# Seven half-size products per pair of gate tiles, in a transformer trunk on one Trainium2 core

## The reference, cut to what matters

```
for l in range(DEPTH):
    h = rmsnorm(x, norm_mix[l])
    z = h @ w_in[l]                       # 1024 -> 3608 columns
    q, kc, vc, ks, vs, kw, vw, nsa_g, u, g_a, g_s = jnp.split(z, split_at, axis=-1)
    o_a = nsa_mixer(q, ...)               # three attention branches: compressed, selected, window
    o_b = s5_mixer(u, ...)                # diagonal state space, then a GLU
    merged = jax.nn.sigmoid(g_a) * (o_a @ proj_nsa[l]) + jax.nn.sigmoid(g_s) * (o_b @ proj_s5[l])
    x = x + merged @ w_out[l]
    x = x + hier_moe(rmsnorm(x, norm_ffn[l]), ...)   # 32 experts, 96 matrices of 2 MB in each layer
```

## Time and profile before

| What | Value |
|---|---|
| Time, median of 3 runs (lowest, highest) | 1862.13 us (1861.97, 1865.38) |
| Span of the profiled execution | 1861.1 us, 21432 instructions |
| TensorE busy | 1689.1 us, 91% |
| VectorE busy | 553.4 us, 30% |
| ScalarE busy | 391.6 us, 21% |

### The profile page before, as it was taken

The page is one execution under the profiler, slowest core; times in us unless marked ns, Lnnn a source line. Parts: engine busy times, 40 slices in busy tenths (PEclk is TensorE's granted clock), DMA queues, the critical chain, the costliest instruction groups (busy, mean ns, idle before and its releaser), DMA issues. The chain is left out here.

```text
span 1861.1 us, 21432 instructions
## 1 busy us (share of the span) xinstructions
PE 1689.1 (91%) x7466; PEld 817.6 (44%) x7466; DVE 553.4 (30%) x1678; ACT 391.6 (21%) x967; POOL 81.9 (4%) x157
## 2 busy tenths in 40 slices
PE   8999999999998778788999999999999987778788
PEld 6664444445443323233477644444544432333233
DVE  4872345435000000000378713463340000000003
ACT  3323344111111111111132234440111111110111
POOL 1000000000010000000000000000001100000000
PEclk9999999999999999998999999999999998999999
DMA  5641110463999999999938211004659999999997
GB/s 168 157 132 46 33 36 23 181 249 127 398 427 426 428 426 427 426 427 427 389 104 223 66 46 46 24 23 181 249 197 412 427 426 427 425 427 428 425 427 332
DMA packets 121903, 496.39 MB, mean 267 GB/s; under 512 B 42036, under 2 KB 78900, under 8 KB 94160
## 3 DMA queue, kind: packets, MB, share of 16 engines
q1 hardware_dynamic: 109584, 472.75, 64.0%
q0 software_dynamic: 8928, 16.52, 2.4%
q10 hardware_dynamic: 3296, 5.84, 0.8%
HBM read 489.25 MB, written 30.47 MB: 279 GB/s over the span
## 5 line engine op out<-in xcount | busy, mean ns | idle before, releaser
L1104 PE MATMUL bank<-arena 128*64 128x512 f32 x2176 | 692.5, 622 | 93.4 <-DMA arena<-in_expert_up 31.7
L1104 PEld LDWEIGHTS bank<-arena 128*64 128x64 f32 x2176 | 229.6, 143 | 358.8 <-issue 358.6
L2034 DVE SCALAR_TENSOR_TENSOR arena<-bank,halves,arena 128x512 f32<-128x512 f32 x32 | 24.0, 751 | 814.6 <-PE bank L1104 814.6
L779 PE MATMUL bank<-hT,arena 128*128 128x512 f32 x512 | 262.0, 611 | 4.1 <-ACT arena L1344 3.5
L1104 PE MATMUL bank<-h,arena 128*64 128x512 f32 x320 | 140.0, 614 | 24.2 <-DMA arena<-in_expert_gate 9.7
L1104 PE MATMUL bank<-spare_slot,arena 128*64 128x512 f32 x320 | 134.7, 618 | 28.9 <-DMA arena<-in_expert_gate 9.0
L754 PE MATMUL bank<-arena,hT 128*128 128x256 f32 (+1 forms) x512 | 118.0, 387 | 3.1 <-DMA arena<-in_w_in 2.3
L1104 PE MATMUL bank<-hT,arena 128*64 128x512 f32 x256 | 120.7, 627 | 0.0
L997 PE MATMUL bank<-arena,hT 128*128 128x512 f32 x256 | 115.0, 597 | 0.0
L779 PEld LDWEIGHTS bank<-hT,arena 128*128 128x128 f32 x512 | 83.4, 192 | 52.2 <-issue 44.3
L754 PEld LDWEIGHTS bank<-arena,hT 128*128 128x128 f32 x512 | 95.6, 190 | 19.4 <-DVE hT L1570 2.7
(11 more groups left out here) (366 smaller groups left out, 1638.8 us busy)
## 6 DMA issues: line engine op xcount, KB each, us to landing
arena<-in_expert_up SPq DMA_DIRECT2D x48, 2048.0 KB, 34.1
arena<-in_expert_gate SPq DMA_DIRECT2D x44, 2048.0 KB, 36.1
arena<-in_expert_down SPq DMA_DIRECT2D x44, 2048.0 KB, 40.4
arena<-in_w_in SPq DMA_DIRECT2D x26, 1024.0 KB, 7.1
spare_slot<-in_expert_gate SPq DMA_DIRECT2D x8, 2048.0 KB, 30.0
h<-in_expert_gate SPq DMA_DIRECT2D x8, 2048.0 KB, 31.6
hT<-in_expert_up SPq DMA_DIRECT2D x8, 2048.0 KB
spare_slot<-in_expert_down SPq DMA_DIRECT2D x8, 2048.0 KB, 37.9
```

The source lines that it names most:

```text
L779: r = pe.matmul(bank[:, FB, :], lhs, rhs, start=(k == 0), stop=last)
L1104: r = pe.matmul(dst[CAP * e:CAP * e + CAP, :], moving[:, k, CAP * e:CAP * e + CAP], w, start=(k == 0), stop=(k == n - 1))
L2034: STT(hid, bank[:, 3, :], slot_root, hid, ALU.mult, ALU.mult).then_inc(act_ready, 1)
```

## The change

Four of the sixteen gate tiles (`PLAIN = 2` pairs) stay as they are. The other twelve are taken as six pairs (`FAST = 6`). For a pair the weights are a 2x2 block matrix (low and high half of the 1024 rows by first and second tile), the tokens a 2x2 block matrix (low and high rows by early and late 256 tokens), and the product is made by Strassen's scheme in Winograd's form: seven products, each of four matmuls of 128x128 against 256 tokens, in place of sixteen matmuls against 512.

- Sums of tokens (`token_sums`, four, 128x1024 each) are made once per layer by VectorE, three into the dead query part of `h`, one in place in `hT`.
- Sums of weights (`weight_sum`, four per pair, 128x512 each) are made by VectorE ahead of the pair.
- The products run in four stages, (1, 6), (2, 7), (4, 5), (3), each one filler group in the bank. After stage 0 ScalarE copies the bank into `fast_p` (in `spare_slot`) and VectorE adds one half into the other; after the others VectorE adds the bank to what is there (`half_sums`: 512 columns after stage 1, 512 and 256 after stage 2, 256 after stages 0 and 3), and right behind it makes the next pair's weight sum s + 1.
- The tanh of a fast pair is taken later, by ScalarE from SBUF (`tanh_fast`), and the merge waits for it (`gate_ready`).
- `fill` counts in units of a 256-column product; 100 are done ahead of the loop (nine groups), 48 + 98 in it, 2 behind it. The 24 entries of `FILL_AT` are chosen so that every group in the loop but the last ends in the call in front of `scores(n + 1)`.
- The fast pairs' chunks alternate between ring slots 0 and 2; slots 1 and 3 hold the sums of weights. `load(0)` and `load(1)` of the experts wait for all half sums as well.

```
-FILL = [("gate", i) for i in GATES[:8]] + [("z", m) for m in range(4)] + [("gate", i) for i in GATES[8:]]
-FILL_AHEAD = 52
-FILL_AT = [5, 4, 3, 2]
+STAGES = ((1, 6), (2, 7), (4, 5), (3,))
+FILL = [("gate", i) for i in GATES[:2 * PLAIN]]
+FAST_STAGES = [("fast", j, s) for j in range(FAST) for s in range(4)]
+FILL += FAST_STAGES[:18] + [("z", 0)] + FAST_STAGES[18:20] + [("z", m) for m in range(1, 4)] + FAST_STAGES[20:]
+RING_AT = [0, 1, 2] + [3, 3] + [3, 2] + [0, 2] * (FAST // 2) + [1, 0, 2]
+FILL_AT = [8, 6, 2, 6, 6, 6,
...
+            def filled_before(i):
+                g = FILL[i - 1]
+                if i and g in BY_ACT:
+                    pe.wait_ge(fill_evac, BY_ACT[g])
+                elif i:
+                    pe.wait_ge(half_sum, BY_DVE[g])
...
                 for n in range(len(UNITS)):
-                    rest = fill(FILL_AT[UNITS[n][0]] - 1, one_group=True)
+                    fill(FILL_AT[n])
                     if n + 1 < len(UNITS):
                         scores(n + 1)
-                    fill(rest)
                     values(n)
...
+                def half_sums(j, s):
+                    m = fast_gates(j)
+                    both = bank[:, FB, :]
+                    if s == 0:
+                        dve.wait_ge(fill_evac, BY_ACT[("fast", j, 0)])
+                    else:
+                        dve.wait_ge(fill_done, FIDX[("fast", j, s)] + 1)
...
+                    if s == 0:
+                        r = TT(late, fast_p[:, EARLY], late, ALU.add)
+                    elif s == 1:
+                        r = TT(gates[:, m, :], fast_p, both, ALU.add)
...
+                    r.then_inc(half_sum, 1)
+                    if j + 1 < FAST:
+                        weight_sum(j + 1, s + 1)
...
                 chunk_scan()
+                token_sums(1, 2)
+                weight_sum(0, 1)
...
+                token_sums(4, 3)
                 sums_qk(NT)
...
                 for n in range(len(UNITS)):
+                    add_fills(2 * n)
                     weigh(n)
...
+                    add_fills(2 * n + 1)
```

More of the change, by code:

```diff
@@ L115, with tanh_at @@
 GATE_S5_AT = FILL_STEP[FIDX[("z", 3)]] // 2 + 1
+BY_ACT = {g: i + 1 for i, g in enumerate(g for g in FILL if g[0] != "fast" or g[2] == 0)}
+BY_DVE = {g: i + 1 for i, g in enumerate(FAST_STAGES)}
 def fills_ending(step):
-    return [i for i in range(FILLED, len(FILL)) if FILL_STEP[i] == step]
+    return [g for i, g in enumerate(FILL) if i >= FILLED and FILL_STEP[i] == step]
+def tanh_at(step):
+    return [j for j in range(FAST) if FILL_STEP[FIDX[("fast", j, 3)]] + 2 == step]
 def key_tiles(unit):
@@ new lines, in fill @@
+            def fill(cost):
+                while cost > 0 and filled[0] < len(FILL):
+                    i, k = filled
+                    kind, m = FILL[i][:2]
+                    if k == 0:
+                        filled_before(i)
+                    if kind == "fast":
+                        stage = STAGES[FILL[i][2]]
+                        r = fast_product(m, stage[k // (KD // 2)], k % (KD // 2))
+                        each = 1
+                    else:
+                        if kind == "gate":
+                            w = chunk(5 + GATES.index(m) // 2)
+                            lhs, rhs, n = w[:, k, P * (m % 2):P * (m % 2) + P], hT[:, k, :], KD
+                        else:
+                            pe.wait_ge(gelu_done, 2)
+                            lhs, rhs, n = w_glu[:, k, P * m:P * m + P], gT[:, k, :], 2
+                        r = pe.matmul(bank[:, FB, :], lhs, rhs, start=(k == 0), stop=(k == n - 1))
+                        each = 2
+                    last = (k + 1) * each == fill_cost(FILL[i])
@@ L782, in fill @@
                     filled[:] = [i + 1, 0] if last else [i, k + 1]
-                return 0
+                    cost -= each
             def group(g, tap=None):
@@ L1349, in evac_fill, with tanh_fast, evac_fills @@
                 r.then_inc(fill_evac, 1)
+            def tanh_fast(j):
+                act.wait_ge(half_sum, BY_DVE[("fast", j, 3)])
+                for k in range(2):
+                    g = gates[:, fast_gates(j) + k, :]
+                    act.activation(g, g, ACT.Tanh, scale=0.5).then_inc(gate_ready, 1)
+            def evac_fills(step):
+                for g in fills_ending(step):
+                    if g in BY_ACT:
+                        evac_fill(g)
+                for j in tanh_at(step):
+                    tanh_fast(j)
             def table_of(function, n):
@@ L1474, in _ @@
                         evac_heads(n)
-                for i in fills_ending(2 * len(UNITS)):
-                    evac_fill(i)
+                for step in range(2 * len(UNITS), 2 * len(UNITS) + 3):
+                    evac_fills(step)
                 enter(act, exp_clear, l)
```

183 lines of the change are left out of this document (134 added, 49 removed).

## The result

The changed kernel takes 1902.4 us (median of 4 runs, 1901.7 to 1906.3), the kernel before, beside it, 1862.1 us: ratio 1.0213 with a 95% interval of 1.0198 to 1.0227. It is slower, by 40.3 us between the medians, 39.7 by the ratio and 38.8 between the profiled spans. The forecast was +37.4 us and 1899.5 us. A fourth run of the kernel before took 2855.5 us and is left out as a slow one.

What follows compares the result with a forecast made beforehand. TensorE's own order ahead of the merge was taken as the bounding path. Per layer -8.8 + 28.3 - 0.8 = +18.7 us, twice +37.4, giving 1899.5 us; range 1868 to 1916, the forecast's own 1886 to 1911.

Steps and rivals of the forecast that it cites:

- The hold: Attention loop: VectorE's half and weight sums stand ahead of the softmax scalings, so TensorE's turns wait; +28.3 us per layer.
- Its steps at unit 8: From P, when TensorE issues the scores: scalings start at P + 1.42, turn ends 1.77 later; a wait of 2.3 us.
- short fillers: Loop units 13, 16, 17: in two, one full-width matmul less covers the exponentials; 1.0 us in all, an estimate.
- units 2 and 10: Loop units where TensorE was to wait for the late scalings, 1.8 us at unit 2 and 1.2 at unit 10.
- unit 19: Loop unit whose longer filler was to cover a wait already there, against a hold of 0.9 us: zero.
- The clock: Rival: TensorE's pauses in the loop lower its clock to 0.95, +8 us per layer, 1915 us; chance 0.05.
- A clock below 1.00 in the loop: Attention loop: one of the listed signs that would show the forecast wrong; no size given.
- The products: TensorE's gate matmuls: six pairs at 12.26 us each instead of 13.73, -8.8 us per layer.
- The waits between groups: TensorE's idling for bank evacuation: 3.25 us per layer before, 2.45 after, net -0.8.
- four waits: S5 stretch: waits at group ends for ScalarE or VectorE evacuation, 0.41, 0.50, 0.84 and 0.23 us, together 1.98.
- The sums did not hide: Denies a rival: scalings late in no loop unit, only products and group waits count, 1843 us; chance 0.13.
- a late ring: Rival: weight chunks landing above 8 us delay weight sum and scalings at three places per layer, 1911 us; chance 0.06.

Runs made afterwards that it cites:

- e1: Changed kernel with VectorE taking the softmax scalings (`weigh`) ahead of the half sum and weight sum: 1846.6 us, ratio 0.9924 to the kernel before.
- e5: Changed kernel with four unused matmuls added in the long pauses ahead of the first turns of units 11, 14 and 23: 1895.9 us, ratio 1.0174.
- e4: Changed kernel with all VectorE sums left out and ScalarE reading out every group, so gates are not completed: 1838.3 us, ratio 0.9877.
- e2: Changed kernel with the weight sums in the loop moved behind the next unit's extrema, half sums still ahead of the scalings: 1881.0 us, ratio 1.0101.
- e3: Changed kernel with one more unused 512-column VectorE maximum behind each weight sum, ahead of the scalings: 1942.8 us, ratio 1.0438.

## Why the prediction was right

**The hold, the term that decides.** Its mechanism is shown by e1: with the scalings first, the pauses of 42.6 us are 0.8, and 55.8 us go. Its steps at unit 8 came out within 0.01 us. Its size per layer was forecast at 28.3, of which 1.0 is for short fillers. It is read from the length of the loop in layer one, from the first scores to the first projection behind the loop. The rows are the changed kernel, e5 (the same, with the clock at 1.00) and e4 (the same products without sums):

```profile
180.40:359.58 179.18, 156.29 (x876) 0.97 0.11 30
...
181.63:356.47 174.84, 157.24 (x900) 1.00 0.11 31
...
180.51:328.90 148.39, 146.36 (x877) 1.00 0.13 36
```

VectorE's sums make the loop 174.84 - 148.39 = 26.5 us longer (26.5 in layer two as well), where 27.3 were forecast. The rows of the pauses alone show less: (42.6 - 0.8) / 2 = 20.9 us, and 3.35 for turns at the pace of the scalings (64.5 us busy in e5, 57.8 in e1), together 24.3. A row's pause begins at the modelled end of the matmul before it, and without a hold the turn would start earlier than that, as at unit 8, so these rows show too little. By distances of starts the long holds came out as forecast at other units too: from P to the next filler 3.55 us at unit 11 and 3.78 at unit 14 in e5, for 3.57 and 3.80. Too high were units 2 and 10, by 0.4 each, since their turns are late in e4 as well; too low was unit 19, 0.8 where nothing was forecast. The short-filler units 13, 16 and 17 show no pause, but their turns end 0.3, 0.3 and 0.9 us later behind P than before, 1.5 for the 1.0 forecast; such turns are in e4 too, and so in its -9.8 below and not in the 26.5.

**The clock, a rival at 0.05, happened as well.** I had priced it at 8 us per layer as an average of 0.95; it was a clock of 0.97, at three places per layer, 3.3 to 4.3 us per layer (e5). "A clock below 1.00 in the loop" stood among the signs that would make the forecast wrong. The rival was right as a mechanism and too large as a price; in the sum the clock stood at nothing. By its measured parts the change costs 26.5 - 9.8 - 1.25 us and 3.3 to 4.3 for the clock, 18.8 to 19.8 us per layer; it costs 19.4 (spans) to 20.1 (medians), and 18.7 were forecast. The hold with its short fillers, the products and the waits were forecast 1.8, 1.0 and 0.45 us too dear, and the clock made up for it. So the total is nearer than its terms were, and part of that is luck.

**The products.** Forecast -8.8; alone they bring -9.8 (e4), since a group of few long passes and one of more short ones start alike: in the S5 stretch four passes of 256 columns and two of 512 both take 1.06 us from start to next start, and at unit 8 twelve passes of 256 take 238.87 - 236.17 = 2.70 us, 0.225 each, where six of 512 took 2.68, 0.447 each. At these two prices the six pairs give 6 x (32 x 0.447 - 56 x 0.225) = 10.2 us, an estimate. That reason is read from rows and was not run apart.

**The waits between groups.** Forecast -0.8. The trace has 4.0 us in all (2.2, 0.8 and 1.0) for 6.5, so -1.25 per layer. In the S5 stretch four waits were priced, 1.98 us together. Three show, 0.33, 0.42 and 0.75, and the fourth does not, so 1.5:

```profile
157.83 1.13 PE L847 MATMUL bank<-hT,arena 128*128 128x256 f32 x4 [0.33 <-ACT spare_slot L1435]
...
164.43 1.13 PE L847 MATMUL bank<-h,arena 128*128 128x256 f32 x4 [0.42 <-DVE arena L1960]
...
171.45 0.92 PE L847 MATMUL bank<-hT,arena 128*128 128x256 f32 x3 [0.75 <-DVE spare_slot L1965]
```

**What stays open.** Products that are fed by VectorE's sums bring less than products alone even with the scalings first: e1 is 4.1 us per layer above e4. Of this the loop has 3.1 (151.46 for 148.39 us) and the S5 stretch 0.3. By distances of starts 2.5 us lie directly behind the first turns, where the next filler waits for a half sum in e1 and for nothing in e4 (at unit 23, 2.50 for 1.82 us from the last group's start to the next filler); the rows of waits show 1.65 of it (6.5 us for 3.2 in both layers). The rest was not placed. Nor is it known why some pauses are followed by a lower clock and others are not.

**The other rivals.** The sums did not hide (42.6 us of pauses). Nothing waited for a late ring. The weight loads hid under products of half the width. Against the Trainium skill ("TensorE: Matmul & The Clock Gate", Part 3, "The mechanism"), by whose list loads overlap only across different row groups, these full-height products keep nearly the forecast's pace (0.225 for 0.219 us at unit 8), and e4 is faster than the kernel before; the same section also names a background weight buffer, which would allow it. On the clock the same page's section "Loop structure matters more than you think" was borne out in its direction: e5 differs from the changed kernel by work in the pauses alone, and it wins back 6.5 us. The page's case is a long wait for DMA, and the pauses here are some 2 us long.

## What to carry to other kernels

A cheap operation on a lightly used engine costs what waits behind it in that engine's queue. VectorE had time for every sum here, and the same sums cost 55.8 us more in front of the softmax scalings than behind them, where they cost 8.3 (e1 against e4). Put an operation that waits for TensorE behind those that TensorE itself will wait for, and look at the order within a unit, never at the busy share of a stage.

Price a pause in TensorE's stream together with the matmuls behind it. When a forecast is hit, check its terms all the same, and measure them by distances of starts: the idle times of the rows made this hold look 2 us per layer smaller than it was.

## What was not expected of the hardware

The granted clock fell behind single pauses of 2.01 to 2.10 us in an otherwise dense loop, and four passes of 256 columns then took 1.70 us for 0.86. The length of the pause alone does not decide. The lower clock also followed pauses of 1.71 us (unit 8, layer two) and, in e2, 1.50 us (unit 14, layer two). It did not follow pauses of 1.96 us (unit 5) and 2.07 us (unit 11, layer two) in the changed kernel. In e3 one of 2.17 us at unit 0 was followed by windows at 0.84 and 0.82, and one of 2.79 us at unit 11 by full pace and a clock of 1.00:

```profile
278.76 1.03 PE L1035 MATMUL bank<-ident,arena 128*128 128x128 f32 x4 [2.79 <-DVE arena L2037]
279.62 1.03 PE L847 MATMUL bank<-hT,arena 128*128 128x256 f32 x4
```

```profile
275.00:280.00 5.00, 2.21 (x14) 1.00 0.00 0
280.00:285.00 5.00, 4.80 (x28) 1.00 0.00 0
```

What else enters was not tried, and each kernel has one profiled execution. A reader can rely on the pair of the changed kernel and e5 as wholes: with work in three pauses per layer neither loop shows a lower clock, and 6.5 us are won. No length of a pause, and no one unit, can be relied on.
